# Keys and values projected before the queries in a hybrid encoder layer, with semaphores cleared as ranges and the residual input loaded in four parts

## What is computed

```python
h = _rms(x, lw['norm1_g'])
proj = h @ lw['w_in']
p_rwkv, q, k, v, qm, gates = jnp.split(proj, _split_points(IN_SIZES), axis=-1)
o_a, s_new, shift_new = _rwkv(p_rwkv, ...)
q = _rms(q.reshape(B, T, SWA_HEADS, SWA_HD), lw['swa_qn_g'])
k = _rms(k.reshape(B, T, SWA_KV_HEADS, SWA_HD), lw['swa_kn_g'])
o_b = _swa_prompt(q, k, v, lw['swa_sink'])          # sample: with cached keys and values
qm = _rms(qm.reshape(B, T, MEM_HEADS, MEM_HD), lw['mem_qn_g'])
o_m = _mem_attend(qm, mem_k, mem_v).reshape(B, T, MEM_W)
br = jnp.einsum('btnc,ncd->btnd', jnp.stack([o_a, o_b, o_m], axis=2), lw['w_branch'])
gt = jax.nn.sigmoid(gates.reshape(B, T, N_BRANCH, D_MODEL))
x = x + jnp.sum(gt * br, axis=2) @ lw['w_out']
h = _rms(x, lw['norm2_g'])
a_in, u = jnp.split(h @ lw['w_up'], 2, axis=-1)
x = x + (jax.nn.gelu(conv(a_in)) * u) @ lw['w_down']
```

## Time and profile before

| | us |
|---|---|
| time, median of 3 runs | 2172.36 (2170.70 to 2173.53) |
| time of the profiled execution | 2172.47 |
| its span, first to last instruction | 2170.6 |
| PE busy | 2039.1 (94%) |
| DVE busy | 1218.9 (56%) |
| POOL busy | 1144.0 (53%) |
| ACT busy | 968.4 (45%) |

### The profile page before, as it was taken

The page is one execution under the profiler, slowest core; times in us unless marked ns, Lnnn a source line. Parts: engine busy times, 40 slices in busy tenths (PEclk is TensorE's granted clock), DMA queues, the critical chain, the costliest instruction groups (busy, mean ns, idle before and its releaser), DMA issues. The chain is left out here.

```text
span 2170.6 us, 40374 instructions
## 1 busy us (share of the span) xinstructions
PE 2039.1 (94%) x15646; PEld 1922.4 (89%) x15646; DVE 1218.9 (56%) x2213; ACT 968.4 (45%) x1951; POOL 1144.0 (53%) x916
## 2 busy tenths in 40 slices
PE   5999899899999999989998999999989898899998
PEld 5988788799999998868887999999978787899998
DVE  6297765555665215866545466632298765557740
ACT  5455333435444434543343444444455334355542
POOL 5643233365666654333334666666644344667775
PEclk9999999999999999999999999999999999999999
DMA  5522222463344442222226533444421223744443
GB/s 171 166 73 63 68 82 86 140 205 119 122 132 144 152 130 91 74 68 69 82 95 193 159 122 122 130 149 141 157 87 62 86 81 107 228 137 144 151 151 127
DMA packets 158525, 264.04 MB, mean 122 GB/s; under 512 B 20096, under 2 KB 53632, under 8 KB 158336
## 3 DMA queue, kind: packets, MB, share of 16 engines
q1 hardware_dynamic: 157760, 260.42, 37.9%
q10 hardware_dynamic: 576, 1.05, 0.1%
HBM read 241.95 MB, written 19.46 MB: 120 GB/s over the span
## 5 line engine op out<-in xcount | busy, mean ns | idle before, releaser
L215 POOL TENSOR_TENSOR k_w_lo<-k_raw,k_w_hi 128x512 fp32r<-128x512 f32 x832 | 1097.5, 1331 | 922.7 <-ACT k_w_hi L206 869.3
L206 ACT ACTIVATE k_w_hi<-k_raw 128x512 fp32r<-128x512 f32 x832 | 501.6, 618 | 357.9 <-PE k_acc L237 131.3
L235 PE MATMUL k_acc<-k_x_hi,k_w_hi 128*128 128x384 f32 (+1 forms) x1152 | 403.9, 351 | 18.6 <-PEq L70 10.1
L236 PE MATMUL k_acc<-k_x_lo,k_w_hi 128*128 128x384 f32 (+1 forms) x1152 | 380.2, 330 | 0.0
L237 PE MATMUL k_acc<-k_x_hi,k_w_lo 128*128 128x384 f32 (+1 forms) x1152 | 379.9, 330 | 0.0
L235 PEld LDWEIGHTS k_acc<-k_x_hi,k_w_hi 128*128 128x128 f32 x1152 | 220.1, 191 | 38.8 <-issue 22.7
L236 PEld LDWEIGHTS k_acc<-k_x_lo,k_w_hi 128*128 128x128 f32 x1152 | 220.4, 191 | 2.8 <-issue 0.5
L237 PEld LDWEIGHTS k_acc<-k_x_hi,k_w_lo 128*128 128x128 f32 x1152 | 220.1, 191 | 0.0
L235 PE MATMUL k_acc<-k_o_hi,k_w_hi 128*128 128x384 f32 (+1 forms) x288 | 99.1, 344 | 30.5 <-PEq L70 13.9
L235 PE MATMUL k_acc<-g0f_xg_hi,k_w_hi 128*128 128x384 f32 x352 | 117.9, 335 | 2.2 <-DVE g0fu_a_raw L2114 2.2
L235 PE MATMUL k_acc<-g1f_xg_hi,k_w_hi 128*128 128x384 f32 x352 | 117.9, 335 | 2.2 <-DVE g1fu_a_raw L2114 2.2
(11 more groups left out here) (753 smaller groups left out, 4391.5 us busy)
## 6 DMA issues: line engine op xcount, KB each, us to landing
k_raw<-w_up SPq DMA_DIRECT2D x264, 256.0 KB, 2.6
k_raw<-w_gate SPq DMA_DIRECT2D x144, 256.0 KB, 3.2
k_raw<-w_down SPq DMA_DIRECT2D x96, 256.0 KB, 3.5
k_raw<-w_rwkv SPq DMA_DIRECT2D x84, 256.0 KB, 2.6
k_raw<-w_branch SPq DMA_DIRECT2D x72, 256.0 KB, 3.5
k_raw<-w_attn SPq DMA_DIRECT2D x60, 256.0 KB, 3.1
k_raw<-w_out SPq DMA_DIRECT2D x48, 256.0 KB, 3.0
k_raw<-w_down_end SPq DMA_DIRECT2D x24, 256.0 KB, 3.4
```

The costliest lines, as they stand in the source:

```text
L206: act.activation(c.w_hi[s][:, 0:n], c.raw[s][:, 0:n], ACT.Copy).then_inc(c.hi_done, 1)
L215: pool.tensor_tensor(c.w_lo[s][:, 0:n], c.raw[s][:, 0:n], c.w_hi[s][:, 0:n].bitcast(F32), ALU.subtract).then_inc(c.lo_done, 1)
L235: pe.matmul(out, wh, xh, start=(u.begins and k == 0), stop=False)
L236: pe.matmul(out, wh, xl, start=False, stop=False)
```

## The change

Five things change. Semaphores of a block are cleared as ranges of consecutive numbers. In `pa` the keys and the values (tiles 4 and 5) are projected first. The keys' norm, the turns of the values, `kq` and `v_tok` move from after the last `pa` tile, or from the attention, to steps of the chain beside the queries' projections; the preparation of attention has eight steps instead of six, and attention one less. The distances are new. In the FFN block SP waits before each gate for that gate's store only, and `x1` comes in four parts after branch units 2, 5, 8 and 11, each behind a wait for all stores. In the diff the lists of distances are cut to the steps up to the first item, and `exps` and `m_exps`, which move as they are, are left out.

```diff
     def __exit__(self, *exc):
         out = self.stack.__exit__(*exc)
-        for sem in self.sems:
-            self.nc.gpsimd.sem_clear(sem)
+        nums = sorted(sem.num for sem in self.sems)
+        first = 0
+        for i, num in enumerate(nums):
+            if i + 1 == len(nums) or nums[i + 1] != num + 1:
+                self.nc.gpsimd.sem_clear(range(nums[first], num + 1))
+                first = i + 1
         return out
...
+A_ORDER = (4, 5, 0, 1, 2, 3, 6, 7, 8, 9)
...
     for g in range(len(GROUPS)):
         for stage, w, n in (("pa", a["w_attn"], A_TILES), ("pr", a["w_rwkv"], R_TILES), ("gate", a["w_gate"], 3 * DT)):
-            for m in range(n):
+            for m in A_ORDER if stage == "pa" else range(n):
                 for u in halves(stage, g, m, w[m]):
                     add(*u)
...
 DISTANCES = (
-    (1, 2, 2, 8, 30, 1, 1, 2, 1, 1, 2, 0, 0, 4, 0, 0, 4, 4, 2, 0, 0, 0, 0, 3, 1, 2, 4, 0, 2, 0, 0, 0, 0, 4, 0, 0,
...
-    (42, 2, 1, 2, 1, 1, 2, 0, 0, 4, 0, 0, 4, 1, 3, 0, 0, 4, 0, 1, 0, 3, 1, 1, 4, 0, 0, 0, 0, 4, 0, 0, 4, 3, 0, 3,
...
-    (43, 3, 1, 2, 1, 2, 1, 0, 2, 4, 0, 0, 0, 5, 0, 5, 0, 0, 0, 2, 1, 2, 1, 2, 2, 0, 0, 0, 0, 2, 0, 0, 2, 4, 0, 2,
...
+    (1, 2, 2, 10, 2, 1, 3, 3, 19, 2, 0, 0, 6, 0, 4, 2, 0, 2, 3, 1, 0, 0, 2, 0, 3, 1, 2, 4, 0, 2, 0, 0, 2, 0, 2, 0,
...
+    (15, 3, 3, 4, 18, 2, 1, 1, 2, 0, 6, 0, 0, 4, 1, 3, 0, 0, 4, 0, 1, 0, 3, 1, 1, 4, 0, 0, 2, 0, 2, 0, 0, 2, 4, 2,
...
+    (15, 3, 3, 4, 18, 4, 2, 1, 1, 3, 5, 0, 0, 0, 5, 0, 2, 0, 1, 2, 2, 1, 2, 1, 2, 2, 0, 0, 0, 0, 3, 0, 0, 1, 5, 0,
...
-N_PREP, N_POST, N_ATTN_PREP = 14, 9, 6
+N_PREP, N_POST, N_ATTN_PREP = 14, 9, 8
...
-    n_attn = 1 + 3 + 3 + sum(4 + 4 * (p + 1 < n_items) + 2 for p in range(n_items))
+    n_attn = 3 + 3 + sum(4 + 4 * (p + 1 < n_items) + 2 for p in range(n_items))
...
             def attn_prep():
+                pe.wait_ge(S["a_squared"], 1)
+                pe.matmul(bank[5][:, 0:T], c.ones_head[:, :], asq[:, 4, 0:T], start=True, stop=True).then_inc(S["a_rows"], 1)
+                yield
+                yield
+                yield
+                pe.wait_ge(S["a_root"], 1)
+                pe.wait_ge(c.acc_read, tile_of(c, g, "pa", 5) + 1)
+                if g > 0:
+                    pe.wait_ge(S["before"], 2 if g == LAST else 1)
+                if g == LAST:
+                    pe.wait_ge(S["cache"], 64)
+                for b in blocks:
+                    mm = pe.transpose(bank[4 + b // 4][:, b % 4 * P:(b % 4 + 1) * P], vw[:, b * P:(b + 1) * P],
+                                      c.ident[:, :])
+                mm.then_inc(S["v_turned"], 1)
+                yield
+                pe.wait_ge(S["v_tok"], 1)
                 pe.wait_ge(S["a_squared"], 9)
-                pe.matmul(bank[5][:, 0:T], c.ones_head[:, :], asq[:, 4, 0:T], start=True, stop=True).then_inc(S["a_rows"], 1)
                 for j in range(4):
                     rows = slice(32 * j, 32 * j + 32)
                     mm = pe.matmul(bank[0][rows, 0:T], c.ones[:, 0:32], asq[:, 5 + j, 0:T], start=True, stop=True)
                 mm.then_inc(S["q_rows"], 1)
                 yield
-                yield
                 pe.wait_ge(S["q_read"], 1)
                 for n, b in enumerate((4, 0)):
                     for p, it in enumerate(items):
                         mm = pe.transpose(bank[b][0:it.nq, p * P:(p + 1) * P], q_rows[:, n, it.q0:it.q0 + it.nq], c.ident[:, :])
                 mm.then_inc(S["q_turned"], 1)
-                yield
                 yield
                 yield
                 yield
...
             def attn():
-                pe.wait_ge(S["a_root"], 1)
                 pe.wait_ge(S["q_root"], 1)
-                if g > 0:
-                    pe.wait_ge(S["before"], 2 if g == LAST else 1)
-                if g == LAST:
-                    pe.wait_ge(S["cache"], 64)
-                for b in blocks:
-                    mm = pe.transpose(bank[4 + b // 4][:, b % 4 * P:(b % 4 + 1) * P], vw[:, b * P:(b + 1) * P],
-                                      c.ident[:, :])
-                mm.then_inc(S["v_turned"], 1)
-                yield
                 pe.wait_ge(S["kq"], 1)
                 scores(0, 0)
                 yield
                 scores(0, 1)
                 yield
-                pe.wait_ge(S["v_tok"], 1)
                 m_scores(0)
                 yield
...
             def attn_prep():
                 if g > 0:
                     act.wait_ge(c.stored, 16 * DT * g)
-                act.wait_ge(S["q_rows"], 1)
-                act.activation(q_rows[:, 0, 0:T], bank[4][:, 0:T], ACT.Copy)
-                act.activation(q_rows[:, 1, 0:T], bank[0][:, 0:T], ACT.Copy).then_inc(S["q_read"], 1)
                 yield
                 rsqrt_act(act, c, axs[:, 0:T], at_[:, 0:T], ay[:, 0:T], S["a_root"], 1)
                 yield
                 yield
-                rsqrt_act(act, c, qxs, qt, qf, S["q_root"], 1)
-                yield
-                yield
-                yield
...
-            def attn():
                 act.wait_ge(S["a_done"], 1)
...
                 ins.then_inc(S["v_tok"], 1)
                 yield
+                act.wait_ge(S["q_rows"], 1)
+                act.activation(q_rows[:, 0, 0:T], bank[4][:, 0:T], ACT.Copy)
+                act.activation(q_rows[:, 1, 0:T], bank[0][:, 0:T], ACT.Copy).then_inc(S["q_read"], 1)
+                yield
+                yield
+                rsqrt_act(act, c, qxs, qt, qf, S["q_root"], 1)
+                yield
+                yield
...
+            def attn():
                 yield
                 yield
                 exps(0)
...
                 dve.tensor_scalar(axs[:, 0:T], bank[5][:, 0:T], 1.0 / 64, RMS_EPS, ALU.mult, ALU.add).then_inc(S["a_root"], 1)
                 yield
                 yield
+                rsqrt(dve, axs[:, 0:T], at_[:, 0:T], ay[:, 0:T], S["a_root"], 1)
+                dve.wait_ge(S["a_root"], ROOT)
+                kn = vec(c, "kn")
+                ins = dve.scalar_tensor_tensor(kw[:, WINDOW:WINDOW + prompt], pa[:, 4, 0:prompt], kn, ay[:, 0:prompt],
+                                               ALU.mult, ALU.mult)
+                if g == LAST:
+                    ins = dve.scalar_tensor_tensor(kw[:, 2 * WINDOW + prompt:2 * WINDOW + T], pa[:, 4, prompt:T], kn,
+                                                   ay[:, prompt:T], ALU.mult, ALU.mult)
+                ins.then_inc(S["a_done"], 1)
+                yield
+                yield
+                yield
                 dve.wait_ge(S["q_turned"], 1)
...
                 ins.then_inc(S["q_root"], 1)
-                rsqrt(dve, axs[:, 0:T], at_[:, 0:T], ay[:, 0:T], S["a_root"], 1)
-                dve.wait_ge(S["a_root"], ROOT)
-                kn = vec(c, "kn")
-                ins = dve.scalar_tensor_tensor(kw[:, WINDOW:WINDOW + prompt], pa[:, 4, 0:prompt], kn, ay[:, 0:prompt],
-                                               ALU.mult, ALU.mult)
-                if g == LAST:
-                    ins = dve.scalar_tensor_tensor(kw[:, 2 * WINDOW + prompt:2 * WINDOW + T], pa[:, 4, prompt:T], kn,
-                                                   ay[:, prompt:T], ALU.mult, ALU.mult)
-                ins.then_inc(S["a_done"], 1)
                 if g < LAST:
                     dve.wait_ge(S["a_done"], 1)
...
                 yield
                 yield
                 rsqrt(dve, qxs, qt, qf, S["q_root"], 1)
-                yield
                 yield
...
                 if g == LAST:
                     dve.wait_ge(S["cache"], 64)
                     dve.tensor_scalar(cmk[:, :, :], cmk[:, :, :], vec(c, "mqn"), None, ALU.mult).then_inc(S["gained"], 1)
-                yield
                 dve.wait_ge(S["q_root"], ROOT)
                 if g == 0:
...
                 if g == LAST:
                     sp.wait_ge(S["a_done"], 1)
+                    sp.wait_ge(S["v_turned"], 1)
                     sp.wait_ge(S["cache"], 64)
                     for dst, src in (("o_kp", kw[:, PROMPT_END:w0]), ("o_vp", vw[:, PROMPT_END:w0]),
...
+X_LOADS = 4
...
                     return
                 if n >= 4:
                     sp.wait_ge(c.acc_read, by["br"][n - 4].tile + 1)
+                sp.wait_ge(c.gate_stored[n % 2], 16 * (g * GATE_STORES + n // 2 + 1))
                 sp.dma_start(gin[:, n % 4, 0:T], c.gates[n, :, 0:T]).then_inc(gate_in[n % 4], 16)
             def dense():
-                for n in range(2):
-                    sp.wait_ge(c.gate_stored[n], 16 * (g + 1) * GATE_STORES)
                 for n in range(3):
                     gate(n)
-                sp.dma_start(x1[:, :, 0:T], a["xT"][:, :, start:start + T]).then_inc(S["x_in"], 16)
                 ended = None
                 for u in us:
                     sp_unit(sp, c, u.index + LEAD)
                     if u.stage == "br":
                         gate(u.m + 3)
+                    if u.stage == "br" and u.m % 3 == 2 and u.m // 3 < X_LOADS:
```

(42 more changed lines are left out.)

## The result

| | before | after |
|---|---|---|
| time, median, us | 2171.95 (2170.70 to 2173.53) | 2143.14 (2140.38 to 2144.77) |
| ratio, 95% interval | | 0.9858 (0.9838 to 0.9879) |
| profiled execution, us | 2172.47 | 2140.38 |
| its span, us | 2170.6 | 2138.5 |
| mean granted clock | 0.980 | 0.982 |

The account below looks back on a forecast made before the run. PE, busy 2039.1 of 2170.6 us, was taken as the bound, so gains could come only from its idle time and low clock. 3.3 + 14.2 + 14.9 - 1.4 = 31.0 us off 2172.47 gave 2141.5 us, range 2131 to 2159.

Parts of the forecast that it names:

- The end: Kernel's end: 48 single clears become one or a few, each range costing one single clear; 3.3 us go.
- FFN blocks: Start of each FFN block: waits after the barrier go, 12.5 us, and one low clock stretch, 1.7; 14.2 in all.
- the waits for the first merges: FFN blocks of groups 0 and 2: PE's waits at L2082 behind ACT's late splits, 1.1 and 1.3 us, would go.
- neither edit would do alone: FFN blocks: an early POOL would meet late loads, early loads a late POOL; only both edits remove the waits.
- Attention: Beginning of attention: the first item's waits go, 11.5 us, and two low clock stretches, 3.4; 14.9, less 1.4 of cost.
- more goes: Rival: later items' waits (4.2 us), group 2's branch stage waits (4.0) and one low stretch may shrink; 2131 us, chance 0.10.
- the held eviction in the key stage: Key stage: DVE's moved chain holds up one eviction, costing 0.45 us for each group, 1.4 us.
- The attention gives its gain back: Rival, attention: if the chain of items is the bound, the wait only moves to a later item; 2156.4 us, chance 0.20.
- A range costs as much as its singles: Rival, clears: 3.3 us at the end and POOL's first waits after barriers stay, 6.0 us; 2147.5 us, chance 0.05.
- the parts starve the branch stage: Rival, FFN branch stage: x1's twelve parts between weight loads make PE idle; slower by over 0.2%, up to 2203 us, chance 0.05.
- The new distances: From the preparation of RWKV on, nearly every chain step keeps its place; counted 0, with 2.1 us per group either way.
- Three low stretches: PE's clock: one low stretch at the FFN blocks, 1.7 us, and two at attention, 3.4 us, would go.

Follow-up runs that it names:

- ranges: The kernel before with one edit, semaphores cleared as ranges: ratio 0.9996 (0.998 to 1.0012), 2174.66 us.
- both: The kernel before with the range clears and the FFN block's edits (gates' own waits, x1 in four parts), attention untouched: ratio 0.9927, 2158.84 us.
- the second trace: A second profiled execution of the changed kernel, nothing altered, measured beside the experiment that puts DVE's keys' norm time back: 2144.07 us.
- eight parts: The changed kernel with x1 in eight parts instead of four, run twice: ratio 0.9829, 2140.16 us, and 0.9842, 2141.43 us.
- all three tries: Attention stretched: kernel before, groups 1 and 2, 1.0075; changed kernel, group 2, 0.9882; changed kernel with eight x1 parts, memory keys' gain moved, group 2's scalings and turns later, 0.987.

## Why the prediction was right, and where its steps were not

The sum came near, but in part by luck: terms missed on both sides nearly cancelled.

**The end.** Forecast 3.3 us, measured 3.0 in the traces; in the time of *ranges* alone it can't be told from noise. The cost of a range was taken as that of a single clear; three took 0.35 us together, the largest 0.63, and that one has cover.

**FFN blocks.** Forecast 14.2 us, measured 12.2 in the first trace, 5.3 in the second, 13.2 in that of *both*. The terms that were named, waits for POOL and late loads, went whole, and *both* shows that they hang on the two edits. They are 10.1 us of waits. What was missed is the remainder: the waits for the first merges, which I had counted as gone with ACT's late splits (1.1 and 1.3 us in the earlier trace rows), did not go. All waits for merges sum to 6.4 us before (1.1, 0 and 5.3 in the three groups) and to 6.4 after (1.0, 1.3 and 4.1), 9.9 in the second trace; why DVE is late there was not looked into. The sentence that neither edit would do alone was right for the ranges and wrong for the parts, which bring half of the waits alone (5.3 of 10.1 us) and 9.5 us by the medians, where *both* gains 16.3 with the end's 3.0. One could have seen it beforehand: POOL, once free, works off a unit in 1.3 us where PE needs 2, so that its lateness costs PE one wait only.

**Attention.** Forecast 14.9 less 1.4, so 13.5; measured 16.5, in the second trace 19.2. The mechanism, DVE's 5 us of keys' norm in the way, is shown by the experiment that puts them back, for 8.2 us. The terms were mis-sized on both sides. The first item's waits were to go whole (11.5 us); 2.6 of them were the scaled scores of group 2, which stayed, with 1.8 more at the second item, and 0.9 and 0.7 us remained in the others. Against that, the waits of the later items in groups 0 and 1 went (2.5 and 1.7 us at L1608 in the earlier trace rows), which I had left to the rival *more goes*, as did two of 1.2 and 1.0 us in 135:215 of group 0 that I had not counted (PE for POOL at L215, PE for DVE at L1647). They stay gone with DVE's time put back; whether the later items' new distances or another moved step took them was not tried. And the held eviction in the key stage (1.4 us) did not show at all. The errors on the two sides nearly cancelled, which is luck.

**The rivals.** *The attention gives its gain back* is false for groups 0 and 1 and right for the mechanism in group 2, where the chain of the items on DVE reads as the bound: there the block gained 3.5 us (5.9 in the second trace) where my terms for it sum to 6.65 (5.4, a low stretch of 1.7, less 0.45). *A range costs as much as its singles* is refuted by its instructions (0.63 us for 110), *the parts starve the branch stage* by eight parts.

**The new distances** were counted at 0. From the first matrix product of the scan to the end of the mix block the three groups take 173.5, 172.2 and 148.0 us, before 171.9, 171.9 and 147.9: 1.9 us more, within the bound. Which of the new distances are needed was not tried: the experiment on the old kernel stretches its lists at another place than the new ones do.

**The clock.** Three low stretches less were forecast, 5.1 us. PE's busy time is 3.7 us lower for the same matmuls, and the mean granted clock 0.982 instead of 0.980. In attention one went instead of two, since group 2's wait stays; at the FFN block of group 1 it moved up to the barrier.

## What to carry to other kernels

When two causes stand in line for the same wait, undo them singly before crediting either: here an early POOL met late loads and gained 1.2 of 10.1 us of waits until the large load left the queue's head. A load that is needed late can be split and put between the urgent ones; here it cost what it delayed the load behind it, not its own bytes. Work moved off a packed in-order engine paid at its evictions; more distance moved the wait or made it longer in all three tries here, and in one of them a wait of 2.8 us became one of 5.6. A second profile is worth taking before a few microseconds are credited to a block: here most waits repeated, the sums of the blocks only within some 7 us.

## What the hardware showed that was not expected

A clear of a range of 110 semaphores takes 630 ns in one instruction, where 110 singles of 44 ns stand 74 ns apart and take 8.1 us. One instruction of DVE, the scaling of the memory scores (128x1024), took 2.18 us for the first item of group 2 and 1.22 for the second in the same execution. The timelines of DVE and POOL have a pattern to it (POOL's second line is two operations run together):

```profile
1571.98 1.27 POOL L223 TENSOR_TENSOR k_w_lo<-k_raw,k_w_hi 128x512 fp32r<-128x512 f32 x1 [9.45 <-ACT k_w_hi L214]
...
1572.15 2.18 DVE L1623 TENSOR_TENSOR g2m_room<-g2m_room 128x1024 f32<-128x1024 f32 x1
...
1597.62 1.22 DVE L1623 TENSOR_TENSOR g2m_room<-g2m_room 128x1024 f32<-128x1024 f32 x1
1597.72 3.77 POOL L223 TENSOR_TENSOR k_w_lo<-k_raw,k_w_hi 128x512 fp32r<-128x512 f32 x2 [3.17 <-ACT k_w_hi L214]
```

Where a `k_w_lo` of POOL is under way when the scaling starts, the scaling ends 1.08 us after POOL's operation and takes 1.96 to 2.32 us; where POOL starts later or not at all, it takes 1.21 to 1.23. Of the 25 scalings of 1024 columns in each trace, 11 are of the first kind before the change and 6 after it, without an exception in either trace. By this pattern an engine that is off the critical path still lengthens the work of one that PE waits for; it was read from traces alone, and what it is worth in time was not tested.
